# Top-256 selection by bit-wise threshold search, packed rotary embedding, and the samples' queries spread by ScalarE

## What is computed

```python
def odd_mixer(x, pool_hist, pos, attn_fn, w_in, c_w, c_scale, w_out):
    h = x @ w_in
    q = partial_rope(h[..., O_Q:O_K].reshape(n, t, N_HEADS, HEAD_DIM), pos)
    k = partial_rope(h[..., O_K:O_V].reshape(n, t, N_HEADS, HEAD_DIM), pos)
    qi = partial_rope(h[..., O_QI:O_KI].reshape(n, t, IDX_HEADS, IDX_DIM), pos)
    ki = partial_rope(h[..., O_KI:O_WI][:, :, None, :], pos)[:, :, 0]
    ...
def index_select(qi, wi, ki_all, pos_q, k_sel):      # k_sel: 256 for the prompt
    score = einsum('nth,nths->nts', wi, relu(einsum('nthd,nsd->nths', qi, ki_all)))
    score = where(admissible, score, -inf)
    return top_k(score, k_sel)
```

## Time and profile before

| | |
|---|---|
| median of three runs | 2930.6 us |
| the profiled execution | 2930.36 us |
| its span on the core | 2928.6 us |
| mean granted TensorE clock | 0.935 |
| slabs 8 to 12 (scores) | about 1353 to 1470 us |
| samples' attention | 1614 to 1729 us |
| prompt's attention | about 1715 to 1966 us |

### The profile page before, as it was taken

The page is one execution under the profiler, slowest core; times in us unless marked ns, Lnnn a source line. Parts: engine busy times, 40 slices in busy tenths (PEclk is TensorE's granted clock), DMA queues, the critical chain, the costliest instruction groups (busy, mean ns, idle before and its releaser), DMA issues.

```text
span 2928.6 us, 42085 instructions
## 1 busy us (share of the span) xinstructions
PE 2621.6 (90%) x15608; PEld 2426.1 (83%) x15608; DVE 1554.8 (53%) x1866; ACT 861.1 (29%) x1362; POOL 1035.5 (35%) x752
## 2 busy tenths in 40 slices
PE   7899979999999999789986866579799999999995
PEld 7899969999999999677686223359699999999995
DVE  2522266455254253547877889961664651542544
ACT  2211153122122122424721234551532221221223
POOL 2222653433232235715834000005533332332355
PEclk9999979999999999789998875799799999999997
DMA  3111101211111111121022420001012111111111
...
DMA packets 65100, 148.55 MB, mean 51 GB/s; under 512 B 6922, under 2 KB 31050, under 8 KB 64746
## 3 DMA queue, kind: packets, MB, share of 16 engines
...
## 4 chain that ended last, share of the span: by engine, by line
PE 74%; DVE 10%; issue 8%; POOL 5%; ACT 2%; DMA 1%; POOLq 1%; SPq 0%; DVEq 0%; ACTq 0%
PE PS L467 23%; PE PS L470 23%; PE PS L468 23%; DVE SCT L1627 3%; POOL SCT L1282 2%; POOL WL L1166 1%; DVE m8b L1629 1%; DVE m8a L1629 1%; POOL Z L1232 1%; DVE PS L1739 1%; PE PS L679 1%; PE PS L700 1%; PE PS L724 1%; PE PS L548 0%; PE PS L529 0%
## 5 line engine op out<-in xcount | busy, mean ns | idle before, releaser
L468 PE MATMUL PS<-XL,WH 128*128 128x352 f32 x3168 | 1027.5, 325 | 0.0
L467 PE MATMUL PS<-XH,WH 128*128 128x352 f32 x2976 | 968.6, 326 | 32.9 <-POOL WL L1166 17.8
L1166 POOL TENSOR_TENSOR WL<-RAW,WH 128x1024 fp32r<-128x1024 f32 x210 | 532.1, 2535 | 1056.9 <-ACT WH L813 1056.9
L470 PE MATMUL PS<-XH,WL 128*128 128x352 f32 x2976 | 647.2, 326 | 0.0
L467 PEld LDWEIGHTS PS<-XH,WH 128*128 128x128 f32 x2976 | 566.0, 190 | 59.7 <-issue 42.0
L468 PEld LDWEIGHTS PS<-XL,WH 128*128 128x128 f32 x3168 | 601.4, 190 | 0.0
L470 PEld LDWEIGHTS PS<-XH,WL 128*128 128x128 f32 x2976 | 514.5, 190 | 0.0
L813 ACT ACTIVATE WH<-RAW 128x1024 fp32r<-128x1024 f32 x210 | 223.4, 1064 | 608.4 <-PE PS L470 587.4
L467 PE MATMUL PS<-HH,WH 128*128 128x352 f32 x1056 | 341.8, 324 | 17.7 <-POOL WL L1166 13.7
L468 PE MATMUL PS<-HL,WH 128*128 128x352 f32 x1056 | 341.2, 324 | 0.0
L1420 DVE SCALAR_TENSOR_TENSOR cv<-ext,fpar,cv 128x1072 f32<-128x1072 f32 x88 | 287.6, 3268 | 12.3 <-DVE cv L1416 0.2
...
## 6 DMA issues: line engine op xcount, KB each, us to landing
...
KP<-in_ck SPq DMA_DIRECT2D x32, 256.0 KB, 3.3
VP<-in_cv SPq DMA_DIRECT2D x32, 256.0 KB, 2.9
...
kix<-in_kidx SPq DMA_DIRECT2D x32, 64.0 KB, 1.8
```

The lines of the kernel that those rows point to most:

```text
L467: pe.matmul(o, WH[j][:, k, :], hi[:, k, c * TW:(c + 1) * TW], start=first, stop=False)
L468: pe.matmul(o, WH[j][:, k, :], lo[:, k, c * TW:(c + 1) * TW], start=False, stop=False)
L470: mm = pe.matmul(bank_set(j)[:, c, :], WL[j][:, k, :], hi[:, k, c * TW:(c + 1) * TW], start=False, stop=last)
L1166: pool.tensor_tensor(WL[j][:, :, :], RAW[j][:, :, :], WH[j][:, :, :].bitcast(F32), ALU.subtract).then_inc(w_lo, 1)
```

## The change

Three things are done together.

1. **Search.** The 32 rounds of `max` and `match_replace` become a search for the 256th largest score, bit by bit. Each of 32 steps counts, for three blocks (groups (2, 3, 4) and (5, 6, 7)), the scores at or above a candidate (`tensor_scalar` with `accum_out`, its marks going to an unused `mark` of bytes), then two small instructions on 128x3 numbers keep or reject the bit and set the next. Each pass waits for all counts before it. Three items at the end of each group handle ties (six instructions per block) and write the bias. An item is now one pass on one block. The first group starts in slab 10, its ties fall into slab 20; the second group ends with its ties beside pair 12; no item lies beside pairs 13 to 31.
2. **Rotary.** ScalarE empties a slab straight into its place. The 32 rows that turn are gathered by two DMAs on ScalarE's queue into a packed tile `pk`, one group of four slabs at a time; VectorE turns the packed tile once per group (four times instead of thirteen); SP's queue scatters the rows back, two DMAs per slab. The gather of a group waits for the scatter of the one before. The rotary tables come as 16 DMAs instead of 2. All sample index dots now stand in slab 7 instead of at the end of slab 6 and in slab 7.
3. **Samples' queries.** The eight copies into `QB` go from VectorE, behind the last pooling, to ScalarE, behind the output of the pooling state and the clearing of `QB`.

```diff
+        GROUPS = ((2, 3, 4), (5, 6, 7))
+        PASSES = 32 * 3
+        BEST = PASSES + 3
+        ROUNDS = len(GROUPS) * BEST
+        slab_rounds = {9: 0, 10: 12, 11: 13, 12: 13, 13: 13, 14: 9, 15: 9, 16: 9, 17: 8, 18: 5, 19: 5, 20: 4, 21: 3}
+        slot_rounds = [7] * 8 + [3] * 13 + [0] * 19
...
+            def scatter(x, rows):
+                sp.wait_ge(roped, x + 1)
+                for c in range(ROPES[x][1]):
+                    for half in range(2):
+                        p = 32 * c + 16 * half
+                        sp.dma_start(rows(c)[64 * half:64 * half + 16, :], pk[p:p + 16, :]).then_inc(scattered, 16)
+            scatter(0, lambda c: KI)
             stream(IN1 + 4, IN1 + S_K, IN1 + 18)
             stream(IN1 + S_K, IN1 + S_Q, IN1 + 12)
+            scatter(1, lambda c: QI[:, c, :])
             stream(IN1 + S_Q, IN1 + S_V, IN1 + 8)
+            scatter(2, lambda c: K[:, c, :])
             stream(IN1 + S_V, IN1 + S_P, IN1 + 4)
+            scatter(3, lambda c: Q[:, c, :])
...
             for dst, name in ((RC, "rc"), (RS, "rs")):
-                act.dma_start(dst[:, :], io[name]).then_inc(rope_in, 16)
+                for p in range(0, P, 16):
+                    act.dma_start(dst[p:p + 16, :], io[name][0:16, :]).then_inc(rope_in, 16)
...
+            def gather(s, x, row):
+                c = s - ROPES[x][0]
+                wait_emptied(act, IN1 + s)
+                act.wait_ge(scattered, moved(x))
+                for half in range(2):
+                    p = 32 * c + 16 * half
+                    act.dma_start(pk[p:p + 16, :], row[64 * half:64 * half + 16, :]).then_inc(gathered, 16)
...
+            act.wait_ge(scattered, moved(4))
+            act.wait_ge(qb_zero, 1)
+            for h in range(HEADS):
+                half = slice(64 * (h % 2), 64 * (h % 2) + 64)
+                act.activation(QB[half, h // 2, :, DEC * h:DEC * h + DEC],
+                               Q[half, h // 2, NP:NT].rearrange("p (s q) -> p s q", s=SEQS), ACT.Copy).then_inc(qb_set, 1)
...
+            def rotate(x):
+                w = 32 * ROPES[x][1]
+                dve.wait_ge(rope_in, 256)
+                dve.wait_ge(gathered, moved(x + 1))
+                dve.stream_shuffle(sh[0:w, :], pk[0:w, :], [p ^ 8 for p in range(32)]).then_inc(shuf, 1)
                 dve.wait_ge(shuf, x + 1)
+                dve.tensor_tensor(pk[0:w, :], pk[0:w, :], RC[0:w, :], ALU.mult).then_inc(rcos, 1)
+                dve.tensor_tensor(sh[0:w, :], sh[0:w, :], RS[0:w, :], ALU.mult).then_inc(shufs, 1)
+                dve.wait_ge(rcos, x + 1)
                 dve.wait_ge(shufs, x + 1)
+                dve.tensor_tensor(pk[0:w, :], pk[0:w, :], sh[0:w, :], ALU.add).then_inc(roped, 1)
...
+                    dve.wait_ge(counted, at0)
+                    dve.tensor_scalar(mark[:, 0:P * (blocks[x] + 1)], sc, bound, None, ALU.is_ge, ALU.add,
+                                      accum_out=cnt[:, x:x + 1]).then_inc(counted, 1)
+                    if x < 2:
+                        return
+                    dve.wait_ge(counted, at0 + 1)
+                    dve.tensor_scalar(rej[:, :], cnt[:, :], float(TOPK_P), -1.0 if step == 0 else 2.0 ** bit,
+                                      ALU.is_lt, ALU.mult).then_inc(rejected, 1)
+                    dve.wait_ge(rejected, 32 * g + step + 1)
...
+                        dve.scalar_tensor_tensor(cand[:, :], rej[:, :], 1 << (bit - 1), cand[:, :], ALU.bitwise_xor,
+                                                 ALU.bitwise_xor).then_inc(stepped, 1)
...
+                    dve.tensor_scalar(mark[:, 0:n], sc, bound, None, ALU.is_le, ALU.add, accum_out=cnt[:, x:x + 1]).then_inc(tied, 1)
+                    dve.tensor_scalar(eqs[:, 0:n], sc, bound, -FAR, ALU.is_equal, ALU.mult).then_inc(tied, 1)
+                    dve.tensor_scalar(ties0[:, :], cnt[:, x:x + 1], float(n - TOPK_P), FAR, ALU.subtract, ALU.mult).then_inc(tied, 1)
+                    dve.tensor_tensor_scan(sc, eqs[:, 0:n], eqs[:, 0:n], ties0[:, :], ALU.add, ALU.bypass).then_inc(tied, 1)
+                    dve.scalar_tensor_tensor(eqs[:, 0:n], sc, 0.0, eqs[:, 0:n], ALU.is_le, ALU.mult).then_inc(tied, 1)
+                    dve.scalar_tensor_tensor(sc, mark[:, 0:n], FAR, eqs[:, 0:n], ALU.mult, ALU.add).then_inc(mb_set, 1)
...
+            rotate(1)
+            dve.wait_ge(scattered, moved(2))
             blocked(lambda half, h: QIB[half, :, DEC * h:DEC * h + DEC], QI, qib_zero, qib_set)
...
+            sample_best(range(0, TOPK_S // 8))
             sample_bias()
             slab_best(9)
+            rotate(2)
             for c in range(4):
                 slab_best(S_Q + c)
+            rotate(3)
...
-            dve.wait_ge(roped, S_V + 2)
-            blocked(lambda half, h: QB[half, h // 2, :, DEC * h:DEC * h + DEC], Q, qb_zero, qb_set)
```

More of the change, by code:

```diff
@@ L22 @@
 U32 = mybir.dt.uint32
+U8 = mybir.dt.uint8
 P = 128
@@ L259, in build @@
             sem("s_" + n) for n in ("dots", "relu", "head_sums", "scores", "top", "last", "bias"))
-        dot_mm, dot_relu, sc_acc, sc_barred, top_, mb_set, mb_early = (
-            sem("i_" + n) for n in ("dots", "relu", "scores", "barred", "top", "bias", "causal_bias"))
+        dot_mm, dot_relu, sc_acc, sc_barred, counted, rejected, stepped, tied, mb_set, mb_early = (
+            sem("i_" + n) for n in ("dots", "relu", "scores", "barred", "counted", "rejected", "next_bound", "ties", "bias", "causal_bias"))
         k_in = [sem("key_pages_in0"), sem("key_pages_in1"), sem("key_pages_in2")]
@@ L366, in build, with moved @@
         S_UNIT = 8
+        ROPES = ((S_KI, 1), (S_QI, 4), (S_K, 4), (S_Q, 4))
+        def moved(x):
+            return 32 * sum(n for _, n in ROPES[:x])
         def added(u):
@@ L383, in build @@
             n = ahead(p)
-            if n and n % 8 == 0 and n // 4 in (2, 4, 6):
-                assert start_round[SEQS + p] >= 2 * BEST * (n // 8), (p, n)
+            if n in (8, 20):
+                assert start_round[SEQS + p] >= BEST * (1 + n // 20), (p, n)
         @block.sync
@@ L992, in rectified @@
                     act.activation(dst, r[:, x, 0:w], ACT.Copy, scale=wtok[:, b, h:h + 1]).then_inc(weighted, 1)
-            feature_slab(S_KI)
+            feature_slab(S_KI, KI[:, :])
+            gather(S_KI, 0, KI)
             feature_slab(S_WI)
@@ L997, in _ @@
             act.dma_start(wis.rearrange("s h q -> h s q"), qf[1][0:HEADS, NP:NT].rearrange("p (s q) -> p s q", s=SEQS)).then_inc(wi_out, 16)
-            feature_slab(S_QI)
+            feature_slab(S_QI, QI[:, 0, :])
+            gather(S_QI, 1, QI[:, 0, :])
             act.wait_ge(wi_out, 16)
@@ L1006, in _ @@
                         rectified(KD * (s - S_UNIT) + k)
-                feature_slab(s, HD ** -0.5 if s >= S_Q else 1.0)
+                x = 1 if s < S_K else 2 if s < S_Q else 3
+                row = (QI, K, Q)[x - 1][:, s - ROPES[x][0], :]
+                if s == S_Q:
+                    act.wait_ge(sb_set, 2)
+                feature_slab(s, row, HD ** -0.5 if s >= S_Q else 1.0)
+                gather(s, x, row)
+            act.dma_start(io["o_ki"], KI[0:IDX, :]).then_inc(kv_out, 16)
             act.dma_start(io["o_k"], K[:, :, :]).then_inc(kv_out, 16)
-            act.dma_start(io["o_ki"], KI[0:IDX, :]).then_inc(kv_out, 16)
             for s in range(S_V, S_P):
@@ L1616, in best @@
             def best(u):
-                r, second = u // 2, u % 2
-                blocks = GROUPS[r // BEST]
-                if r % BEST == 0 and not second:
-                    dve.wait_ge(sc_barred, blocks[-1] - 1)
-                for x, b in enumerate(blocks):
-                    if u % (2 * BEST):
-                        dve.wait_ge(top_, 2 * u - 1 + x)
-                    if second:
-                        dve.match_replace(SC[b], m8[x][:, :], SC[b], TAKEN).then_inc(top_, 1)
-                    else:
-                        dve.max(m8[x][:, :], SC[b]).then_inc(top_, 1)
```

109 lines of the change are left out of this document (53 added, 56 removed).

## The result

The changed kernel takes 2892.35 us (median of four runs, 2889.59 to 2893.66), against 2929.57 for the kernel before on the same chip: a ratio of 0.9871, with a 95% interval of 0.9854 to 0.9889. The forecast was 2896.7, within 2866 to 2920. The profiled execution took 2893.66 us, its span is 2891.9 us, which is 36.7 us shorter than before.

A forecast was written before the change was run, and what follows sets the result against it. The slab products hold about 70% of the chain, but VectorE's search sets the attention's pace up to about 1905 us; terms summing to -33.7 on 2930.4 give 2896.7 us, range 2866 to 2920.

The forecast's parts named there:

- The unit costs: VectorE's search: a pass n/0.96 ns + 0.26 us, steps 4.0 and 2.8 us, ties about 11 and 20 us.
- B: Counting passes run at the short tensor-scalar price but hold up GpSimd in slabs 10 to 12; total 2880; chance 0.24.
- D: The search step itself is slower, 6.5 us if a pass takes two cycles a column; total 2960; chance 0.08.
- Pairs 16 to 25: Attention pairs left without search take 58 us instead of 94.9, 3 of it for TensorE's clock: -37 (-45 to -20).
- rival C: Pairs 16 to 25 take 75 us instead of 58, TensorE's clock staying low; total 2914; chance 0.10.
- Pairs 0 to 15: Attention pairs with twelve search steps, the ties and pairs 13 to 15 take 98 us instead of 92: +6.
- Front and slab 7: First scatter ahead of slab 4's weight load: +1; TensorE's stall for the indexer queries in slab 7: +4.3.
- rival E: No measurable change: transfers land behind slab loads, three trips taking 8 us instead of 2; about 2925; chance 0.06.
- Slabs 8 to 12: Four of five rotations vanish, so GpSimd's additions are held up less: -6 (-10 to +5).
- Value copies: Slabs 14 to 16: 27 passes take 25 us where old half-rounds took 19: +1.5 (-3 to +3).
- Samples' start: Query copies leave VectorE, but ties delay the pooling and sample 1's key pages: -2.5 (-12 to +4).
- End of the slots: After sample 7, VectorE's seven passes (9.3 us) are a little shorter than seven half-rounds: -1.

The follow-up runs named there:

- pairs_bare: Changed kernel without the last 36 counting passes and the second group's ties, so no search lies beside any pair; 2844.24 us, one execution.
- ties_spread: Changed kernel with the second group's ties cut into single instructions beside pairs 12, 13 and 16 to 26; 2874.05 us, ratio 0.9801 to the kernel before.
- tables_twice: Changed kernel with the rotary tables loaded by 32 loads of 8 rows instead of 16 of 16 rows; 2882.36 us, one execution.
- dots_later: Changed kernel with the samples' index dots behind chunks 4 and 6 of slab 7 instead of 1 and 4; 2885.20 us, ratio 0.9848.
- rotary_unpacked: Kernel before with the new search and ScalarE's query copies, but the old unpacked rotary, table loads and index dot places; 2888.25 us, ratio 0.9854.
- first_ties_cut: Changed kernel with no search in slabs 20 and 21; the first group's ties, cut into single instructions, go to sample slots 0 and 1; 2884.12 us.
- qb_on_vector: Changed kernel with the eight query copies into QB back on VectorE, behind the last pooling; 2899.51 us, ratio 0.9896.

## Why the prediction was right, step by step

**The unit costs.** Right. VectorE by shape, 1600 to 1830 us (busy us, mean ns, idle before):

```profile
L1676 DVE TENSOR_SCALAR_CACHE_REDUCE mark<-SCT,cand 128x1024 uint8<-128x1024 f32 x31 | 39.6, 1277 | 0.9
L1676 DVE TENSOR_SCALAR_CACHE_REDUCE mark<-SCT,cand 128x896 uint8<-128x896 f32 x31 | 35.3, 1139 | 0.5
...
L1676 DVE DVE_READ_ACCUMULATOR mark<-SCT,cand 128x1 f32 x93 | 7.6, 82 | 0.0
L1681 DVE TENSOR_SCALAR rej<-cnt 128x3 int32<-128x3 f32 x32 | 5.8, 183 | 1.1
...
L1707 DVE TENSOR_TENSOR_SCAN SCT<-eqs,ties 128x1024 f32<-128x1024 bf16 x1 | 2.4, 2350 | 0.0
...
L1709 DVE SCALAR_TENSOR_TENSOR eqs<-SCT,eqs 128x1024 bf16<-128x1024 f32 x1 | 1.2, 1224 | 0.0
...
L1702 DVE TENSOR_SCALAR eqs<-SCT,cand 128x1024 bf16<-128x1024 f32 x1 | 0.7, 748 | 0.0
```

The pass at 896 columns takes 1139 ns and its readout 82; 128 columns more cost 138 ns, 1.08 a column where the forecast had 1.04. From one step of the group (5,6,7) to the next it is 4.05 us (1627.79 to 1631.84), forecast 4.0. The ties take 12.2 us (1579.57 to 1591.81) and 18.9 (1804.11 to 1823.01), forecast 11 and 20. Rivals B and D fall here (B's 39 passes in slabs 10 to 12 are 38). Between the pass with its count (1277 ns) and the tensor-scalar without one (748 ns at the same 1024 columns) lies just the fork between the two prices: I took the maximum for the nearest row, because a count is a reduction. The choice held; that the reduction is the reason is not shown, since the two forms also write different types (bytes and bf16). For B I had drawn on the double rate for tensor-scalar; the Trainium skill, "SBUF — State Buffer", section "Who interferes with whom", itself excepts the form that also writes out its accumulator, which I had missed. The trace agrees with it in both rows, 1277 ns with the accumulator and 748 without.

**Pairs 16 to 25.** Right in size (-38.0 for -37; 56.9 us for 58) and in mechanism: pairs_bare and ties_spread give the same 55.5 us. The 55 that the forecast had without its 3 us for the clock is what these two take; the changed kernel takes 1.4 more. The clock reaches 1.00 there, so rival C falls. No run puts the old search back beside the new rotary and copies; that the search's end is the cause rests on VectorE's rows before and after and on pairs_bare.

**Pairs 0 to 15.** The largest miss, -4.1 for +6. The step that failed is "pairs 13 to 15 are limited by the other engines, 4 to 6 each", 13 of the 98 us. The twelve steps (1740.13 to 1802.88) took 62.8 us, pair 14's maxima and the ties (to 1823.01) 20.1, forecast 65 and 20. But pair 16's logits start 5.1 us behind the ties: the logits of pairs 14 and 15 had been made at 1795.98 and 1801.05, ahead of them, and only what was left of two pairs followed. With two logits buffers a block on VectorE delays the next pairs once, and they don't start again from the beginning behind it.

**Front and slab 7.** The table loads are hidden as said (tables_twice), and the +1 for the scatter is not seen either (-0.2). Slab 4 is emptied 0.2 us earlier than before, so rival E, with 8 us more for each trip, falls. In slab 7 the trip is right to about a microsecond at each station (rotated 1335.45 for 1334.3, QIB set 1343.8 for 1342.7), and TensorE's idle was 4.82 us for 5.8. What the term lacks is the clock: the stall brings it down to 0.64 for the 8 us behind it, some 2.4 us, which dots_later gives back together with the idle; in tables_twice the same stall cost 1.4 us less. Against that, the samples' four head-sum products (2.0 us) now stand behind slab 7 instead of in it, so that they count in slab 8.

**Slabs 8 to 12.** -2.8 for -6, of which +2.1 are the head sums in slab 8; slabs 9 to 12 give -5.0. Cause and size are right, as rotary_unpacked shows. The condition "if the passes block GpSimd too" did not come about: its 512-column additions take 1350 ns in 1375 to 1475 us, 1520 in the kernel before.

**Value copies.** +4.1 for +1.5. The 27 passes take 28.0 us instead of 25: nine steps of 2.86 instead of 2.8, and one small instruction of 128x3 numbers, usually 0.16 us, was held for 2.30 beside GpSimd's split of the weights:

```profile
1522.28 2.30 DVE L1687 SCALAR_TENSOR_TENSOR cand<-rej,cand 128x3 int32<-128x3 int32 x1
```
```profile
1522.15 2.41 POOL L1211 TENSOR_TENSOR WL<-RAW,WH 128x1024 fp32r<-128x1024 f32 x1 [13.31 <-ACT WH L834]
```

The forecast had this collision for large instructions and left the small ones out.

**Samples' start.** Right, -2.1 for -2.5, and station by station. The forecast's times are counted in the kernel before; slab 18 is now emptied 7.8 us later (1560.18 for 1552.35, by the mark and the terms ahead). Less these 7.8, the last pooling ends at 1616.4 (1624.25), sample 1's logits start at 1625.1 (1632.88) and sample 2's at 1639.2 (1647.07); the forecast has 1616, 1624 and 1639. The mechanism is the one that it names: the ties held slab 20's pooling and with it the emptying of slab 21 (1598.79), so that all of slab 21's pooling, 21 us of it, ran beside the residual additions, and sample 1's pages waited for it. Within the term two things work against each other: the ties in slab 20 cost 10 to 12 us (first_ties_cut), and the copies on ScalarE gain 7 to 8 (qb_on_vector). The remark that the move buys little is therefore wrong for the copies by themselves; no number of the sum used it.

**End of the slots.** +2.0 for -1. The -1 for the shorter passes is right; what the term lacks is TensorE's clock, which the forecast put at nothing here. Without the three products that tables_twice names (17.84 us together in the changed kernel), the stretch from sample 2 to pair 2 takes 75.2 us, and in the six other kernels that leave these slots alone 74.9 to 75.3, although with the products they spread over 87.5 to 93.2. The kernel before takes 76.3 and its three products 14.78. So the passes give 1.1 us, and the clock took 3.1.
